# Low parts of the feed-forward weights: from a VectorE subtraction to a ScalarE negation and an adding GpSimd transfer

## What is computed

```python
def conv_glu_ffn(xn, w_up, conv_w, conv_b, w_down):      # D_FF = 2816
    u = xn @ w_up                                         # (512, 1024) @ (1024, 5632)
    u = lax.conv_general_dilated(u, conv_w ..., feature_group_count=2 * D_FF) + conv_b   # 3 taps
    gate, up = jnp.split(u, 2, axis=-1)
    return (jax.nn.silu(gate) * up) @ w_down              # (512, 2816) @ (2816, 1024)

for i in range(DEPTH):                                    # DEPTH = 2
    h = h + mix
    h = h + conv_glu_ffn(rmsnorm(h, ffn_norm_g[i]), w_up[i], conv_w[i], conv_b[i], w_down[i])
    gate = jax.nn.sigmoid(rmsnorm(h, ple_norm_g[i]) @ w_ple_gate[i])
    h = h + gate * (p[i] @ w_ple_proj[i])
return rmsnorm(h, final_norm_g)
```

## Time and profile before

| | |
|---|---|
| median of the three runs | 1099.78 us |
| span of the profiled execution (first to last instruction) | 1097.6 us |
| busy: TensorE, VectorE, ScalarE, GpSimd | 1089.3, 717.1, 515.8, 27.9 us |
| granted TensorE clock, mean | 0.999 of full |
| moved by DMA | 108.1 MB, 99 GB/s on average |

### The profile page before, as it was taken

One profiled execution on the slowest core, in us unless ns is written; L12 is line 12 of the kernel. 1 busy time (PEld: TensorE's weight loads), 2 busy tenths in 40 slices (PEclk: granted clock), 3 DMA queues, 4 the chain that ended last, 5 costly groups with the idle time before them and its releaser, 6 DMA issues.

```text
span 1097.6 us, 14445 instructions
## 1 busy us (share of the span) xinstructions
PE 1089.3 (99%) x5150; PEld 908.0 (83%) x5150; DVE 717.1 (65%) x1101; ACT 515.8 (47%) x776; POOL 27.9 (3%) x86
## 2 busy tenths in 40 slices
PE   9999999999999999999999999999999999999997
PEld 8888888888888888888888889888888888888886
DVE  7567878656775377744777778777437773477636
ACT  6456667554643144421445677444314442244554
POOL 0001101020000000000000000000000000000001
PEclk9999999999999999999999999999999999999999
DMA  9113242322233233332234322233323233223411
GB/s 332 61 58 86 59 96 70 104 92 101 96 96 115 77 96 96 99 116 76 95 106 125 102 89 77 77 96 97 117 77 96 95 103 119 82 92 101 131 62 76
DMA packets 31407, 108.14 MB, mean 99 GB/s; under 512 B 3648, under 2 KB 3648, under 8 KB 31360
## 3 DMA queue, kind: packets, MB, share of 16 engines
q1 hardware_dynamic: 30288, 105.13, 30.7%
q0 software_dynamic: 784, 1.85, 0.7%
q10 hardware_dynamic: 288, 0.53, 0.1%
HBM read 105.39 MB, written 2.11 MB: 98 GB/s over the span
## 4 chain that ended last, share of the span: by engine, by line
PE 97%; DVE 2%; ACT 1%; issue 0%; DVEq 0%; POOL 0%; POOLq 0%
PE bank L1273 31%; PE bank L1275 31%; PE bank L1274 31%; PE bank L1367 1%; PE bank L1293 1%; PE bank L1380 1%; PE bank L1334 0%; PE bank L1560 0%; PE bank L1644 0%; PE bank L1557 0%; DVE probs L950 0%; ACT probs L495 0%; DVE w_lo L828 0%; DVE wT_lo L978 0%; DVE q_lo L934 0%
## 5 line engine op out<-in xcount | busy, mean ns | idle before, releaser
L1273 PE MATMUL bank<-x_hi,w_hi 128*128 128x512 f32 x896 | 350.3, 391 | 0.0
L1275 PE MATMUL bank<-x_hi,w_lo 128*128 128x512 f32 x896 | 348.8, 389 | 0.0
L1274 PE MATMUL bank<-x_lo,w_hi 128*128 128x512 f32 x896 | 348.7, 389 | 0.0
L828 DVE TENSOR_TENSOR w_lo<-w_raw,w_hi 128x1024 fp32r<-128x1024 f32 (+1 forms) x189 | 225.8, 1196 | 43.2 <-ACT w_hi L393 43.1
L393 ACT ACTIVATE w_hi<-w_raw 128x1024 fp32r<-128x1024 f32 (+1 forms) x189 | 193.7, 1030 | 109.7 <-PE bank L1275 109.5
L1275 PEld LDWEIGHTS bank<-x_hi,w_lo 128*128 128x128 f32 x896 | 168.2, 188 | 35.3
L1273 PEld LDWEIGHTS bank<-x_hi,w_hi 128*128 128x128 f32 x896 | 168.2, 188 | 35.0 <-DVE x_lo L836 0.4
L1274 PEld LDWEIGHTS bank<-x_lo,w_hi 128*128 128x128 f32 x896 | 168.2, 188 | 34.5
L1273 PE MATMUL bank<-g_hi,w_hi 128*128 128x512 f32 x352 | 136.9, 389 | 0.0
L1274 PE MATMUL bank<-g_lo,w_hi 128*128 128x512 f32 x352 | 136.9, 389 | 0.0
L1275 PE MATMUL bank<-g_hi,w_lo 128*128 128x512 f32 x352 | 136.9, 389 | 0.0
(11 more groups left out here) (220 smaller groups left out, 1171.8 us busy)
## 6 DMA issues: line engine op xcount, KB each, us to landing
w_raw<-in_weights SPq DMA_DIRECT2D x189, 512.0 KB, 3.5
gain_and_h<-in_xT SPq DMA_DIRECT2D x7, 256.0 KB, 5.7
o_inv<-o_rows POOLq DMA_DIRECT2D x7, 256.0 KB, 4.6
out<-emb SPq DMA_DIRECT2D x3, 512.0 KB, 3.0
p_raw<-in_pT SPq DMA_DIRECT2D x1, 1024.0 KB, 10.1
w_raw<-in_weights SPq DMA_DIRECT2D x2, 256.0 KB, 3.8
gain_b<-in_final_gain SPq DMA_DIRECT2D x1, 512.0 KB, 4.1
gain_and_h<-in_gain_and_x ACTq DMA_DIRECT2D x1, 260.0 KB, 3.6
```

The lines of the kernel that those rows point to most:

```text
L828: dve.tensor_tensor(w_lo[s][:, 0:w], w_raw[s][:, 0:w], w_hi[s][:, 0:w].bitcast(F32), ALU.subtract).then_inc(lo_done, 1)
L1273: pe.matmul(dst, w1, m1, start=start and i == 0, stop=False)
L1274: pe.matmul(dst, w1, m0, start=False, stop=False)
L1275: last = pe.matmul(dst, w0, m1, start=False, stop=stop and i == len(parts) - 1)
```

## The change

ScalarE's `split_hi` gets a second instruction for a feed-forward unit: it writes minus the high part into `w_lo` (`scale=-1.0`, rounded to float32r like the high part) and counts up `minus_done`. GpSimd waits for it and starts a transfer of the same 512 KB (384 KB for the units of 6 blocks) from HBM into `w_lo` with `accum_op=ALU.add`, so that `w_lo` becomes the weights minus their high part. TensorE waits for that transfer (`low_in` of the slot, 16 for each transfer). VectorE's `split_lo` does nothing for these 136 units and works as before for the other 54. SyncE may overwrite `w_raw` once minus the high part is written; its loop is written out unit by unit. Counts of `lo_done` are taken over the units that are left to VectorE.

```diff
+FFN_UNITS = sum(3 * t for t in FFN_PARTS) - sum(FFN_PARTS) + KT * len(FFN_PARTS)
+FFN_FIRST = [PHASES[f"up{layer}0"][0] for layer in range(DEPTH)]
+def low_by_dma(n):
+    return any(first <= n < first + FFN_UNITS for first in FFN_FIRST)
+def dma_lows(n):
+    return sum(max(0, min(n + 1 - first, FFN_UNITS)) for first in FFN_FIRST)
+def dve_lows(n):
+    return n + 1 - dma_lows(n)
+def low_landed(n):
+    return 16 * sum(1 for k in range(slot_of(n), n + 1, SLOTS) if low_by_dma(k))
...
             for n in range(SLOTS, N_UNITS):          # SyncE, in place of the loops
...
+                if low_by_dma(n - SLOTS):
+                    sp.wait_ge(minus_done, dma_lows(n - SLOTS))
+                else:
+                    sp.wait_ge(lo_done, dve_lows(n - SLOTS))
                 load(n).then_inc(raw_in[slot_of(n)], 16)
...
                 act.activation(w_hi[s][:, 0:w], w_raw[s][:, 0:w], ACT.Copy).then_inc(hi_done, 1)
+                if low_by_dma(n):
+                    act.activation(w_lo[s][:, 0:w], w_raw[s][:, 0:w], ACT.Copy, scale=-1.0).then_inc(minus_done, 1)
...
+            def low_parts(layer):                    # GpSimd
+                for n in range(FFN_FIRST[layer], FFN_FIRST[layer] + FFN_UNITS):
+                    s, w = slot_of(n), blocks_of(n) * P
+                    pool.wait_ge(minus_done, dma_lows(n))
+                    pool.dma_start(w_lo[s][:, 0:w], weights[n, :, 0:w], accum_op=ALU.add).then_inc(low_in[s], 16)
...                                                   # behind the pooling matrices
+            for layer in range(DEPTH):
+                low_parts(layer)
...
                 if n >= N_UNITS:                     # VectorE, split_lo
                     return
+                if low_by_dma(n):
+                    return
...
             def unit(name, u, a, parts, stop=True):  # TensorE
-                pe.wait_ge(lo_done, SLOTS * a + PHASES[name][0] + u + 1)
+                n = PHASES[name][0] + u
+                if low_by_dma(n):
+                    pe.wait_ge(hi_done, SLOTS * a + n + 1)
+                    pe.wait_ge(low_in[slot_of(n)], 16 * a + low_landed(n))
+                else:
+                    pe.wait_ge(lo_done, SLOTS * a + dve_lows(n))
```

More of the change, by code:

```diff
@@ L199, in hybrid_trunk @@
         raw_in = [sem(f"raw_in{s}") for s in range(SLOTS)]
+        low_in = [sem(f"low_in{s}") for s in range(SLOTS)]
+        minus_done = sem("minus_done")
         hi_done, lo_done, unit_done, evac_done = sem("hi_done"), sem("lo_done"), sem("unit_done"), sem("evac_done")
@@ L353, in _ @@
             sp.dma_start(p_raw[:, :, :], pT.rearrange("j p s -> p j s")).then_inc(p_in, 16)
[L354 to L366, removed]
+            for n in range(SLOTS, N_UNITS):
+                if n == PHASES["up00"][0] + 2 * SLOTS:
+                    sp.wait_ge(evac_done, result_of("wo", KT - 1))
+                    sp.dma_start(gain_b[:, :], final_gain[:, :]).then_inc(gain_in, 16)
+                if low_by_dma(n - SLOTS):
+                    sp.wait_ge(minus_done, dma_lows(n - SLOTS))
+                else:
+                    sp.wait_ge(lo_done, dve_lows(n - SLOTS))
                 load(n).then_inc(raw_in[slot_of(n)], 16)
@@ L1499, in embedding @@
                 if m % TT == 0:
-                    pe.wait_ge(lo_done, n + 1)
+                    pe.wait_ge(lo_done, dve_lows(n))
                 if m >= 3:
@@ L1647, in _ @@
             for k in range(KT):
-                pe.wait_ge(lo_done, TAIL + k // 2 + 1)
+                pe.wait_ge(lo_done, dve_lows(TAIL + k // 2))
                 pe.wait_ge(x_ready, KT * NORM_PLE1 + k + 1)
@@ L1668, in _ @@
                     if t == 0:
-                        pe.wait_ge(lo_done, TAIL + TT + k // 2 + 1)
+                        pe.wait_ge(lo_done, dve_lows(TAIL + TT + k // 2))
                     done = gate_product(bank[TT + t][:, :], 1, k, t)
```

## The result

The change makes the kernel 16.5% slower: 1282.93 us in the median of four runs (1273.46 to 1288.55), a ratio of 1.1654 to the kernel before, with a 95% interval of 1.1606 to 1.1703. The forecast was 1158, in a range up to 1250. The remaining 9 us between it and the median are a spread between executions (0.8 us wide before) that no profile here takes apart.

A forecast was written before the change was run, and what follows sets the result against it. The prediction took TensorE, busy 1089.3 of 1097.6 us, as the bound. Up phases 49, last down phases 8 and start of layer 0 1 sum to 58 us, added to the 1099.8 median: 1158 us, range 1108 to 1250.

The forecast's parts named there:

- the start of layer 0: Start of layer 0: GpSimd, busy with pooling matrices until 240.55, lands unit 34's transfer late; 1 us.
- Rival A: Transfer almost as short as a plain load, 3.3 to 4.2 us; kernel 1110 us; chance 0.17.
- Rival C: Not slower: transfer lands within GpSimd's shortest row, 1.7 us; kernel 1100 us; chance 0.03.
- 5.5 us from issue to landing: Adding transfer of 512 KB: 1.4 us ahead of data, 3.36 of data, 0.6 of its 1.68 for the load.
- The high end: Transfer's upper price, from GpSimd's 2.9 us per 256 KB plus 1.1 us for the second stream: 8.6 us.
- 1.4 us ahead of the data: Adding transfer: time from issue at 87.83 to first packets at about 89.2, taken from one earlier transfer.
- I charge nothing: TensorE's clock: no cost, since TensorE stays busy for over 85% in the forecast.
- The budget: Up phases: a transfer may take 3.7 us; each us above delays one lap of three units by 1 us.
- 49 predicted: Up phases of both layers: 82 x (5.5 - 3.7) / 3 = 49 us lost to the transfer.
- a budget of about 14 us: First two down phases: splits wait only for the slot three units earlier, so the transfer costs 0 us.
- the last ones: Last down phase of each layer: 0.7 us left for a 384 KB transfer of 4.7; 4.0 us twice, 8 us.
- rival B: Adding is slow, from 7.5 us; at 8.6 us per transfer the kernel takes 1250 us; chance 0.15.

The follow-up runs named there:

- the copy: The changed kernel with GpSimd's transfer copying the weights into w_lo instead of adding them: 1152.48 us, ratio 1.0487.
- the kernel with the load apart: The changed kernel with SyncE's next load into a slot waiting until the adding transfer has landed: 1220.86 us, ratio 1.1098.
- copy, load apart: The changed kernel with a plain copy instead of the add, and SyncE's loads moved behind its landing: 1142.22 us, ratio 1.0379.
- half the bytes: The changed kernel with the adding transfer covering only the first half of each unit's columns: 1168.92 us, ratio 1.0641.

## Why the prediction was wrong

**The sign, the place and the mechanism were right.** The kernel is slower; the waits stand mostly in the up phases and at the last down phases, released by the transfer. VectorE's relief was worth nothing, the start of layer 0 cost 1.0 us (predicted 1), and the share of PE in an up phase fell to 86 (predicted 90), as the forecast said. Rival A's time, 1110, was that of a transfer of 3.3 to 4.2 us; even the copy took 4.5. The fit of the Trainium skill ("DMA: Bandwidth & Descriptors", SWDGE path), cited beside rival A, gave 3.2 us for 512 KB. The fastest copy of 512 KB here took 3.6, the median one 4.4, the add 7.4. Rival C would have needed 1.7 us.

**The step that failed first was the size of the transfer.** "5.5 us from issue to landing" was chosen between 3.3 and 8.6; it was 7.4. The high end, built from the slope of the issue rows, was nearer than the value built from packets. What the pieces add up to is an add by itself: it lands after 5.5 us where nothing stands beside it. In part that is luck, since the sum had 0.6 us for the load in it and nothing for the 0.3 us between the last packet and the landing. Left out or too small was what stands beside the add. The load costs 1.0 us, not 0.6. The "1.4 us ahead of the data" belongs to the first of the seven transfers back in the kernel before, the quickest of them; the other six show 2.3 to 3.2 us. And the sum has no term for the transfer before on the same queue, which goes with another 0.8 us. By the forecast's own slope of 27.3 laps, 1.9 us more are 52 us.

**The second was "I charge nothing" for the clock.** The argument was that TensorE stays busy for over 85%; it does, and the clock fell all the same. In the up phases of the kernel after, some 165 of the 209 slow distances lie inside units, 36 us over the usual ones; with the slower start of a unit behind a gap it is 41. They stand in the unit at the head of a lap, whose end starts the next transfer of the lap, so that they lengthen it in full. Behind none of the gaps of up to 1.8 us that TensorE has in the up phases of the five kernels below do they stand, behind all of over 2.7 us they do, and in between both are found. A short one, from the kernel with the load apart, in the timeline of an up phase:

```profile
468.22 0.49 PE L1307 MATMUL bank<-x_hi,w_hi 128*128 128x512 f32 x1 [1.68 <-DMA w_lo<-in_weights]
468.55 0.39 PE L1308 MATMUL bank<-x_lo,w_hi 128*128 128x512 f32 x1
468.78 0.40 PE L1309 MATMUL bank<-x_hi,w_lo 128*128 128x512 f32 x1
```

**The budget held.** Landing times and what each lap lost can be set side by side, since five kernels differ in nothing but the transfer and its load. Lost per lap is the up phases' extra time over 27.3 laps.

| kernel | landing, us | lost per lap, us | landing less loss |
|---|---|---|---|
| copy, load apart | 4.4 | 1.29 | 3.1 |
| copy | 4.5 | 1.47 | 3.0 |
| half the bytes | 4.9 | 2.0 | 2.9 |
| add, load apart | 6.2 | 3.7 | 2.5 |
| the kernel after | 7.4 | 5.1 | 2.3 |

The last column is not the budget, since a lap's loss has the clock in it, 0.3 us a lap with the copies and 1.5 in the kernel after. The budget can be read from the laps themselves. In the lap shown above, 5.9 us lie between the end of the unit at its head (503.15) and the negation three units on (509.03), and the two handovers take 0.46 us (509.03 to the issue at 509.49) and 0.22 (landed 516.33, first matmul 516.55). Over the 31 laps of the kernel after whose last unit waited for over 0.3 us, the means are 6.6 us to the negation, 0.6 for the handovers, 7.1 for the landing, and 6.75 for the unit at the head. That leaves a budget of 10.9 - 6.6 - 0.6 = 3.7 us, as forecast, and a lap of 21.0: 3.4 us over 16.3 by the transfer, 1.3 by the slow matmuls. With the copies the same reading, of the fewer units that waited at all, gives 3.1 and 3.35; there ScalarE comes later to its negation (7.0 to 7.3 us), and so they lose more than the forecast's slope gives them.

So the up phases are 49 predicted, 52 for the longer transfer and 41 for the clock: 142, against 139.3 measured.

**The down phases were under-charged.** In the first two, "a budget of about 14 us" holds for units inside the phase, not for its first ones: those are split in a burst at the phase's start (transfers issued at 370.37, 372.37, 376.17 and 378.06 in layer 0), and TensorE idles for 2.55 us ahead of its third unit there (376.94, the transfer having landed at 376.85). 11 us in four phases, where 0 had been said, and where the forecast had named waits as a sign that it was wrong. In the last ones the place was right and the size off. The timeline at the start of layer 1's:

```profile
1182.53 0.83 ACT L416 ACTIVATE w_lo<-w_raw 128x768 fp32r<-128x768 f32 x1
1183.82 0.89 POOL L816 DMA_DIRECT2D w_lo<-in_weights  x1 [7.00 <-ACT w_lo L416]
1191.05 0.77 PE L1307 MATMUL bank<-g_hi,w_hi 128*128 128x512 f32 x1 [5.03 <-issue]
1197.58 0.69 DVE L1083 TENSOR_TENSOR gain_and_h<-bank,gain_and_h 128x512 f32<-128x512 f32 x1 [9.57 <-PE bank L1309]
```

That transfer took 7.1 us, not 4.7. TensorE's gap is 5.0 us, followed by ten slow matmuls at 0.43 us from start to start, which is 2 more. With the units behind it, which were not free as predicted, it makes 11.8.

**From 58 to 174, in one line** (in us): transfer 52, clock in the up phases 41, less 3 that the two sums leave over, first down phases 11, last down phases 15: 116, which is 174 - 58. The high end of the range, 1250, was rival B's 8.6 us with the budget of 3.7 and no clock; the transfer stayed below that, and the time went above it, because the transfer, the clock and the down phases were too low at once and the range moved only the first of them.

## What to carry to other kernels

Work that stands between a late signal and the engine that bounds the kernel is priced by its latency with its spread, not by its bytes: here 136 instructions of 1.2 us, hidden behind TensorE, gave way to transfers of 7.4 us against a budget of under 4, and the idle engine that was freed was worth nothing. If such a transfer must be used, start it one unit earlier (172 of 183 us came back) before trying to make it shorter, and put the work that doesn't need it ahead of the wait. Price a transfer with what is under way beside it: the same add took 5.5 us alone, 6.5 beside a load, and 7.4 in the median of the kernel. In a range, move the terms together that share a cause: a longer transfer also widens gaps, and these cost clock.

## What the runs showed of the hardware

- An adding transfer from HBM into SBUF moves 0.50 MB in 2.5 us with all 16 engines taken, a copy on the same queue 0.52 MB in 1.5 us. The Trainium skill ("Collectives: The Full Stack", part 3) says that the add needs two source reads. The packets go that way: one of 4 KB takes 0.328 us in the add and 0.174 us in the copy, 1.9 times.
- GpSimd's issue of an add occupies it for 0.87 us. The first data come 1.6 us after the issue starts where nothing stands beside the add, and 2.5 to 3 us after it beside a load of 512 KB on the hardware queue.
- An add that starts with a load on the hardware queue lands 1.2 us later in the median than one kept apart from it; a copy 0.1 us later. Why the two differ was not tried. Adds issued while the one before on their queue is still under way land 0.8 to 1.0 us later than the others (7.5 against 6.65 us in the kernel after, 6.8 against 5.8 with the load apart).
- In an otherwise busy kernel, gaps of over 2.7 us on TensorE are followed by six to fourteen matmuls at 0.43 us instead of 0.23, at a granted clock of 0.50; behind gaps of up to 1.8 us the usual distance stands, and between 1.85 and 2.65 us both occur. Useless matmuls in the gaps went with 30 us less time in one placing and nothing in another, which missed most of the gaps.
